# Tokens and the first two weight tiles in quarters, worked off together, with products of ones ahead and squares last

## What is computed

```python
h = rms_norm(x, norm1)                       # over the 2048 columns
z = h @ w_in                                 # 2048 x 5120
u, q, f, i, g = split(z, 1024 columns each)
pool_out = pool_mix(u, ...)                  # windows 2/4/8/16, per-group map, scale
o = hgrn2_recurrence(silu(q), 1 - forget(f), i, log forget(f), state)
x = x + concat(pool_out, norm(o) * silu(g)) @ w_o
h2 = rms_norm(x, norm2)
x = x + (silu(h2 @ w_gate) * (h2 @ w_up)) @ w_down
y = rms_norm(x, norm_f)                      # and the new pooling rows and states
```

## Time and profile before

| | before |
|---|---|
| median of 3 runs | 1475.65 us (1475.46 to 1478.24) |
| profiled execution, its time | 1473.87 us |
| its span, first to last instruction | 1472.1 us |
| PE busy | 1430.2 us, 97% |
| DVE, ACT, POOL busy | 764.2, 575.0, 221.2 us |
| moved by DMA | 214.60 MB, mean 146 GB/s |
| mean granted TensorE clock | 0.988 of full |

### The profile page before, as it was taken

How to read it: one execution, slowest core, us unless ns; L and a number is a source line. 1 busy time by engine, 2 the same in 40 slices (tenths; PEclk the granted TensorE clock), 3 DMA queues, 4 the chain that set the end, 5 groups by cost and what they waited for, 6 DMA issues and landing times.

```text
span 1472.1 us, 26682 instructions
## 1 busy us (share of the span) xinstructions
PE 1430.2 (97%) x9744; PEld 1409.3 (96%) x9744; DVE 764.2 (52%) x1188; ACT 575.0 (39%) x928; POOL 221.2 (15%) x387
## 2 busy tenths in 40 slices
PE   7998999999999999999999999999999999999996
PEld 5998888889999999999999999999999999999996
DVE  5565666667755554444445444444444444444443
ACT  6344445445633343333333333333333333333443
POOL 0263444456312200000000000000000000000131
PEclk9999999999999999999999999999999999999998
DMA  9544445554555555555565554565554556555453
GB/s 247 144 130 132 114 116 144 144 142 121 161 144 142 148 148 151 152 142 134 142 181 142 142 156 124 155 168 146 151 155 125 144 159 171 143 142 149 122 145 111
DMA packets 409521, 214.60 MB, mean 146 GB/s; under 512 B 4093, under 2 KB 407757, under 8 KB 409420
## 3 DMA queue, kind: packets, MB, share of 16 engines
q1 hardware_dynamic: 391207, 203.59, 50.7%
q10 hardware_dynamic: 18277, 10.52, 2.6%
HBM read 206.20 MB, written 7.89 MB: 145 GB/s over the span
## 4 chain that ended last, share of the span: by engine, by line
PE 92%; DVE 3%; POOL 2%; ACT 1%; issue 1%; DMA 1%; DVEq 0%; ACTq 0%; SPq 0%; POOLq 0%
PE bank L382 29%; PE bank L384 29%; PE bank L383 29%; PE bank L522 1%; DVE w_lo L1084 1%; DVE t L1258 1%; DMA xt<-in_x_sample 1%; PE bank L552 1%; PE bank L478 0%; ACT w_hi L711 0%; POOL kp L1606 0%; PE bank L578 0%; ACT tm L849 0%; PE bank L426 0%; POOL km L1597 0%
## 5 line engine op out<-in xcount | busy, mean ns | idle before, releaser
L382 PE MATMUL bank<-a_hi,w_hi 128*128 128x320 f32 x2048 | 641.1, 313 | 0.0
L383 PE MATMUL bank<-a_lo,w_hi 128*128 128x320 f32 x2048 | 636.0, 311 | 0.0
L384 PE MATMUL bank<-a_hi,w_lo 128*128 128x320 f32 x2048 | 635.8, 310 | 0.0
L1084 DVE TENSOR_TENSOR w_lo<-w_raw,w_hi 128x1024 fp32r<-128x1024 f32 (+1 forms) x416 | 459.2, 1144 | 150.8 <-ACT w_hi L711 149.8
L711 ACT ACTIVATE w_hi<-w_raw 128x1024 fp32r<-128x1024 f32 (+1 forms) x416 | 387.9, 968 | 183.2 <-PE bank L384 163.2
L382 PEld LDWEIGHTS bank<-a_hi,w_hi 128*128 128x128 f32 x2048 | 387.4, 189 | 2.1
L383 PEld LDWEIGHTS bank<-a_lo,w_hi 128*128 128x128 f32 x2048 | 387.5, 189 | 0.7
L384 PEld LDWEIGHTS bank<-a_hi,w_lo 128*128 128x128 f32 x2048 | 387.3, 189 | 0.0
L382 PE MATMUL bank<-h_hi,w_hi 128*128 128x320 f32 x704 | 218.5, 310 | 0.0
L384 PE MATMUL bank<-h_hi,w_lo 128*128 128x320 f32 x704 | 217.4, 309 | 0.0
L383 PE MATMUL bank<-h_lo,w_hi 128*128 128x320 f32 x704 | 217.3, 309 | 0.0
(11 more groups left out here) (232 smaller groups left out, 1160.2 us busy)
## 6 DMA issues: line engine op xcount, KB each, us to landing
w_raw<-in_w_gate SPq DMA_DIRECT2D x44, 1024.0 KB, 5.6
w_raw<-in_w_up SPq DMA_DIRECT2D x44, 1024.0 KB, 5.6
w_raw<-in_w_down SPq DMA_DIRECT2D x64, 704.0 KB, 4.8
w_raw<-in_w_in SPq DMA_DIRECT2D x39, 1024.0 KB, 5.8
w_raw<-in_w_o SPq DMA_DIRECT2D x16, 1024.0 KB, 6.1
s<-in_state_hgrn ACTq DMA_DIRECT2D x8, 512.0 KB, 4.8
out<-sn ACTq DMA_DIRECT2D x8, 512.0 KB, 5.2
xt<-in_x_prompt SPq DMA_DIRECT2D x3, 512.0 KB, 9.6
```

The costliest lines, as they stand in the source:

```text
L382: pe.matmul(out, whi[:, par_, cols], r_hi, start=(k == 0), stop=False)
L383: pe.matmul(out, whi[:, par_, cols], r_lo, start=False, stop=False)
L384: last = pe.matmul(out, wlo[:, par_, cols], r_hi, start=False, stop=(k == last_k))
L1084: dve.tensor_tensor(wlo[:, par_, cols], raw[:, par_, cols], whi[:, par_, cols].bitcast(F32), SUB)\
```

## The change

Tokens come in quarters of 512 columns, on twelve semaphores, and the first two weight tiles in quarters of four feature tiles, alternating. PE first multiplies ones by ones (2 products of 512 columns, then, behind the transpose of norm1, 3 more) into a bank nobody reads. Then it turns 3 feature tiles, and works k = 0 to 15 off for units 0 and 1 together, six products for each k. The third token block is padded with zeros (by POOL) to 128 rows, so all three transposes have 128 rows. Units 2 and 3 go to banks of their own (SC, TV), so they need not wait until units 0 and 1 are read; `rms_first` moves to k = 7 of unit 3. The two first squares of ACT move into the k loop (k = 8 and 11), the other four behind it, between the weight halves of units 2 and 3. Weight tile 2 comes in halves, and the cache between them. In the diff, PE waits at k = 0, 4, 8 and 12 for the hi and lo pieces of the quarter; `first_piece` is the piece of 512 columns, on ACT for hi and on DVE in the same place for lo; and the last line is POOL's first. The pooling work from unit 2 on is put in a new written-out order, with the same instructions.

```diff
+            for quarter in range(4):
+                load_x(sp, quarter, 0)
+                if quarter >= 2:
+                    load_x(sp, quarter, 1)
+                for u in range(2):
+                    first_weights(u, quarter)
+            load_params(sp, PARAMS[1:], par_loaded)
+            sp.wait_ge(first_lo, 3)
+            sp.dma_start(w2[:, 0:k_mid, :], win_v[:, 0:k_mid, 2 * P:3 * P]).then_inc(w2_loaded, 16)
             sp.dma_start(cache_t[:, :], cache_pool[0].rearrange("b t c -> (b t) c")).then_inc(cache_loaded, 16)
+            sp.wait_ge(lo_ready, 2)
+            sp.dma_start(w2[:, k_mid:KD, :], win_v[:, k_mid:KD, 2 * P:3 * P]).then_inc(raw_loaded[0], 16)
+            load(3, 1, win_v, (0, KD), 3 * P)
...
-        AHEAD = 8
+        AHEAD = 3
...
-                pe.transpose(b4[:, TP:N], xt[0:NS, 2, k * P:(k + 1) * P], ident[0:NS, 0:NS]).then_inc(xt_t, 1)
+                pe.transpose(b4[:, TP:TP + P], xt[:, 2, k * P:(k + 1) * P], ident).then_inc(xt_t, 1)
+            def keep_busy(count):
+                for _ in range(count):
+                    pe.matmul(OT[:, :].rearrange("p (a b) -> p a b", b=P), ones[:, :],
+                              ones[:, :].unsqueeze(1).to_broadcast([P, 4, P]), start=True, stop=True)
+            pe.wait_ge(fill_done, 1)
+            keep_busy(2)
             pe.wait_ge(ident_loaded, 16)
             pe.wait_ge(norm1_loaded, 16)
             pe.transpose(TK[:, 0:KD], prow[0:KD, :], ident[0:KD, 0:KD]).then_inc(par_t, 1)
+            keep_busy(3)
+            pe.wait_ge(x_pad, 1)
             for k in range(AHEAD):
                 x_transposes(k)
+            for k in range(KD):
                 if k + AHEAD < KD:
                     x_transposes(k + AHEAD)
                 pe.wait_ge(ahi_ready, k + 1)
                 pe.wait_ge(alo_ready, k + 1)
+                for u in range(2):
+                    if k % 4 == 0:
...
+                    out = zb[u][:, 0:N]
+                    pe.matmul(out, whi[:, u, cols], a_hi[:, k, :], start=(k == 0), stop=False)
+                    pe.matmul(out, whi[:, u, cols], a_lo[:, k, :], start=False, stop=False)
+                    last = pe.matmul(out, wlo[:, u, cols], a_hi[:, k, :], start=False, stop=(k == KD - 1))
...
+            unit(U0 + 2, 0, a_rhs, between=(lambda: cache_tiles(0), None), own_bank=SC, read=0)
+            unit(U0 + 3, 1, a_rhs, between=(None, lambda: cache_tiles(1)), after_tile=spread_rms, own_bank=TV, read=0)
+            unit(U0 + 4, 0, a_rhs, between=(fourth_mid, fourth_end), read=1)
...
-            for i in range(2):
-                square(0, i)
+            for u in range(2):
+                first_piece(u, 0)
             act.wait_ge(par_ready, 1)
             for k in range(KD):
...
+                if k % 4 in (1, 2) and k < 12:
+                    first_piece(k % 4 - 1, k // 4 + 1)
                 if k == 8:
+                    square(0, 0)
+                if k == 11:
+                    square(0, 1)
+                if k == 13:
+                    act.wait_ge(w2_loaded, 16)
+                    hi_piece(2, 0, 0, HALF[0])
+            square(0, 2)
+            square(1, 0)
+            act.wait_ge(raw_loaded[0], 32)
+            hi_piece(2, 0, 1, HALF[1])
+            act.wait_ge(raw_loaded[1], 32)
+            hi_piece(3, 1, 0, HALF[0])
+            square(1, 1)
+            square(1, 2)
...
+            pool.memset(xt[NS:P, 2, :], 0.0).then_inc(x_pad, 1)
```

More of the change, by code:

```diff
@@ L30 @@
 HD = D // 2
+QD = D // 4
 TP, NB, TS = 256, 8, 8
@@ L256, in hybrid_kernel @@
         HALF = ((0, 8), (8, 16))
+        QUARTERS = ((0, 4), (4, 8), (8, 12), (12, 16))
         HALF_D = ((0, 8), (8, KB))
@@ L367, in unit @@
             def unit(n, par_, rhs, halves=HALF, between=(None, None), tile_wait=None,
-                     after_tile=None):
-                after(pe, unit_read, n - 1)
+                     after_tile=None, own_bank=None, read=None):
+                after(pe, unit_read, n - 1 if read is None else read)
                 last_k = halves[1][1] - 1
@@ L480, in pool_product, with spread_rms, fourth_mid, fourth_end @@
                     last.then_inc(pool_mm, 1)
[L482 to L498, removed]
+            def spread_rms(k):
+                if k == 7:
+                    rms_first()
+            def fourth_mid():
+                cache_tiles(2)
+                pool_states(0)
+            def fourth_end():
+                pool_states(1)
+                pool_product(0)
+            def sixth_mid():
+                cache_tiles(3)
+                pool_states(2)
+            unit(U0 + 2, 0, a_rhs, between=(lambda: cache_tiles(0), None), own_bank=SC, read=0)
+            unit(U0 + 3, 1, a_rhs, between=(None, lambda: cache_tiles(1)), after_tile=spread_rms, own_bank=TV, read=0)
+            unit(U0 + 4, 0, a_rhs, between=(fourth_mid, fourth_end), read=1)
+            unit(U0 + 5, 1, a_rhs, between=(None, lambda: pool_product(1)), read=2)
+            unit(U0 + 6, 0, a_rhs, between=(sixth_mid, None))
+            unit(U0 + 7, 1, a_rhs, between=(None, lambda: pool_product(2)))
             def sample_thrice(bk, rep):
@@ L714, in _, with first_piece @@
             load_params(act, PARAMS[:1], norm1_loaded)
-            load_x(act, 0, 1)
+            for quarter in range(4):
+                if quarter < 2:
+                    load_x(act, quarter, 1)
+                load_x(act, quarter, 2)
             act.wait_ge(fill_done, 3)
             act.activation(warm[:, 0:1], epst[:, 0:1], ACT.Sqrt)
+            squares = [0]
             def square(half, i):
                 rows, at = (P if i < 2 else NS), 2 * i + half
-                act.wait_ge(x_loaded[half][i], 16)
-                after(act, ss_ready, 3 * half + i)
+                for quarter in range(2 * half, 2 * half + 2):
+                    act.wait_ge(x_loaded[quarter][i], 16)
+                after(act, ss_ready, squares[0])
+                squares[0] += 1
                 act.activation(junk[0:rows, :], xt[0:rows, i, half * HD:(half + 1) * HD], ACT.Square,
                                accum_out=stat[0:rows, at:at + 1]).then_inc(ss_ready, 1)
-            for i in range(2):
-                square(0, i)
+            def first_piece(u, quarter):
+                cols = slice(quarter * QD, (quarter + 1) * QD)
+                act.wait_ge(w_first[u][quarter] if quarter < 3 else raw_loaded[u], 16)
+                ins = act.activation(whi[:, u, cols], raw[:, u, cols], ACT.Copy)
+                if quarter < 3:
+                    ins.then_inc(first_hi, 1)
+                else:
+                    ins.then_inc(hi_ready, 2)
+            for u in range(2):
+                first_piece(u, 0)
             act.wait_ge(par_ready, 1)
@@ L785, in pool_hi @@
                     act.activation(bp_hi[:, j, :], bk[:, 0:N], ACT.Copy, scale=pcol("pool_scale", j)).then_inc(mp_hi_s, 1)
[L787 to L796, removed]
+            cache_copy(0)
+            split_hi(U0 + 4, 0)
+            tail_copy(0)
+            cache_copy(1)
+            split_hi(U0 + 5, 1)
+            cache_copy(2)
+            state_copy(0)
+            tail_copy(1)
+            split_hi(U0 + 6, 0)
+            state_copy(1)
+            pool_hi(0)
+            pool_hi(1)
+            split_hi(U0 + 7, 1)
+            tail_copy(2)
+            cache_copy(3)
+            state_copy(2)
+            split_hi(U0 + 8, 0)
+            pool_hi(2)
             def forget(h, n):
@@ L1134, in lower_bound, with first_piece @@
                 dve.tensor_scalar(lbt[:, 3, :], lbt[:, 4, :], 0.5, 0.5, MUL, ADD).then_inc(lb_ready, 1)
+            def first_piece(u, quarter):
+                cols = slice(quarter * QD, (quarter + 1) * QD)
+                if quarter < 3:
+                    dve.wait_ge(first_hi, 2 * quarter + u + 1)
+                else:
+                    dve.wait_ge(hi_ready, 2 * u + 2)
+                ins = dve.tensor_tensor(wlo[:, u, cols], raw[:, u, cols], whi[:, u, cols].bitcast(F32), SUB)
+                if quarter < 3:
+                    ins.then_inc(first_lo, 1)
+                else:
+                    ins.then_inc(lo_ready, 2)
+            for u in range(2):
+                first_piece(u, 0)
             for k in range(KD):
@@ L1230, in pool_lo @@
                                              in1=bp_hi[:, j, :].bitcast(F32), op0=MUL, op1=SUB).then_inc(mp_lo_s, 1)
[L1232 to L1246, removed]
+            rms_row(1)
+            u_part(0)
+            u_part(1)
+            lo_piece(U0 + 4, 0, 0, HALF[0])
+            u_part(2)
+            lo_piece(U0 + 4, 0, 1, HALF[1])
+            u_part(3)
+            dve.wait_ge(masks_loaded, 16)
+            pool_means(0)
+            lower_bound()
+            split_lo(U0 + 5, 1)
+            pool_means(1)
+            u_part(4)
+            split_lo(U0 + 6, 0)
+            pool_lo(0)
+            u_part(5)
+            pool_lo(1)
+            split_lo(U0 + 7, 1)
+            pool_means(2)
```

(4 more changed lines are left out.)

91 lines of the change are left out of this document (43 added, 48 removed).

## The result

Eight executions of the changed kernel, 1464.65 to 1467.87 us, have a median of **1466.26 us**, against 1475.81 us for eight of before (1471.27 to 1479.33). The ratio is 0.9935, 95% interval 0.9922 to 0.9947: 9.5 us won. The forecast was 1471.4 us and 4.2 us won, in a range from 1466.3.

What follows compares the result with a forecast made beforehand. PE, busy 97% of the span, bounds the kernel. Start 12.7 + loop 19.7 + low clock 2.2 + parameter transpose 0.3 = 34.9 us against 39.05, 4.2 won; on the median of 1475.65 this gave 1471.4 us, range 1466.3 to 1475.0.

Steps and rivals of the forecast that it cites:

- the stalls of the relay: PE waits from a POOL, DVE and ACT relay after a unit is read: six, 15.0 us, and one 4.0; unchanged.
- The mark is 39.05 us: Start of unit 2 in the kernel before, 40.45 us less 1.4 us of PE work that the change moves later.
- its time is 0.12% under the median, and on the median I forecast: Whole kernel: profiled execution 1473.87 us becomes 1469.7; carried to the median of 1475.65, this gives 1471.4 us.
- For as long as in before behind the first product, 4.9 us: Start of the joint loop: low clock level from 12.7 us for 4.9 us, losing 2.2 us.
- the gap before the first product: PE between the ones (over near 9 us) and 12.7 us: only 1.3 to 2.5 us of transposes, so level low.
- Six products are 0.88 + 0.10: Joint k loop: product time per k at full level, 0.10 for the change of kind; a k costs 1.31 us.
- In 8.2 us of transposes alone the level did not rise: Start of the kernel before: 27 transposes ran at the low level, so the low level was assumed at 12.7 us.
- the trace agrees as far as it goes: Start: 27 transposes at the low pace were taken to support the rule that transposes do not count toward full clock.
- the margins at k = 7 of unit 3 and before unit 4: Later units: 3 us spare for 1/rms in unit 3, 0.6 us before unit 4; cost 0, at most 1.
- A: Start: weights land by 9.5 us or the clock carries over; 5.5 to 8 us won, near 1469; chance 0.32.
- B: Start: small transfers run at 190 GB/s, products start at 16.1 us; 0.75 won, 1474.9; chance 0.20 (won under 3).
- C: Later stalls meet other clock moments; three more hit cost 8.7 us against 4.2 won, 1480.1; chance 0.05.

Runs made afterwards that it cites:

- b_same: The kernel before, unchanged, run once more; ratio to before 0.9997.
- a_bridge: The changed kernel with three more products of ones between the transposes of k = 0 and the first joint product; ratio to before 0.9919.
- b_pad: The kernel before with only the third token block padded to 128 rows and its transposes on 128 rows; 1468.58 us, ratio 0.9943.
- a_halves: The changed kernel with tokens and the first two weight tiles in halves, transfers twice as large; ratio to before 0.9957.
- b_ones: The kernel before with only the five products of ones added ahead of the transposes; ratio to before 0.9991.
- b_pad_small: The kernel before with padded transposes and one small 64-row product of ones behind each group of three; 1484.04 us, ratio 1.0047.
- a_rows64: The changed kernel with the third transpose on 64 rows again; ratio to before 0.9953.

## Why the prediction was wrong

Sign and place were right: all that is won is won before unit 2, PE waits nowhere from unit 2 to 7, and the stalls of the relay are the same. The size was not, and four steps have a part in it.

*"The mark is 39.05 us", and "its time is 0.12% under the median, and on the median I forecast".* This step failed most, by 3.5 us. The mark was read from one execution, and I carried its difference to the median, although the start of that kernel depends on when the clock rises. Its start was short because of the very term that the change removes. In b_same the mark is 42.6, and by span and clock 42 of 57 executions go with that trace. Nothing in the one trace said so but a hint that I used the other way round: 27 transposes, and then nine products among further transposes, had passed before the level rose.

*"For as long as in before behind the first product, 4.9 us."* The low level set in at 14 us, not before the first product, and lasted 3.3 us: 1.6 us lost where I had 2.2. That the gap before the first product would cost the level was right (a_bridge fills the gap and keeps it).

*"Six products are 0.88 + 0.10."* The 0.10 for the change of kind was read behind a 64-row transpose. It belongs to the row count: behind padded transposes the first product takes 0.15 us. A k takes 1.21 us instead of 1.31, 1.3 us in thirteen. The padded transposes were right at 0.33.

*"In 8.2 us of transposes alone the level did not rise", and "the trace agrees as far as it goes".* The rule of the Trainium skill ("TensorE: Matmul & The Clock Gate", Part 4), that transposes do not count toward the full clock, does not hold for the float32 transposes of 128 rows here: in b_pad the level rose during transposes alone. The row was read as a statement on all transposes; it was one on groups with a 64-row transpose. So I priced the padding at 0.19 us a group and missed that it gives back a level held low for 15 us or more. It was the part of the change that I gave one sentence.

Right were the first product (12.7 forecast, 13.01 measured), with the slow second weight piece as its cause, that PE sets the pace of the loop, that the margins at k = 7 of unit 3 and before unit 4 hold, and that ones bring nothing over the gap. With pace and level as measured the sum from that trace would have been 5.9 us, inside the range on its own; with the mark of b_same it is 9.5. Of the rivals A came nearest, by neither of its reasons. B was wrong: a_halves shows that smaller transfers win. C did not occur. That the time, 1466.26 us, lies at the very edge of the range is luck: the range was stretched for rival A, not for a baseline that varies.

Not tried: whether 64-row transposes all in a row, with no change of row count, would let the level rise, and whether a small product of 128 rows would hold it down. So why the groups with a 64-row transpose keep it low stays open.

## What to carry to other kernels

Where a profiled stretch runs at TensorE's low level, take a second execution before its length is used in a sum: it may be the part that varies, and a change that ends it wins more than one trace shows. Try equal row counts in a stream of transposes and products; padding 64 rows to 128 took one memset on an idle engine and won 8.4 us here. And an early product is worth more than a warm engine: order the first pieces by when their transfers land.

## What the runs showed that was not expected

- Transposes of 128 rows, nearly back to back, brought TensorE from the low level to the high one: between 9.62 and 15.3 us in b_pad, with no product in between.
- Groups of three with one 64-row transpose went with the low level for 20 us, with PE nearly always busy (b_ones, granted clock 0.50). One added 64-row product for each group of 128-row transposes kept the level low until near 27.6 us (b_pad_small), where b_pad had the high one at 15.3; it cost 15 us, of which 9 or more are the added products.
- A change of row count goes with 0.1 us more in the 64-row transpose and 0.2 us more in the product behind it, at the high level (a_rows64).
- The granted-clock column prints 1.00 until the level first falls from high to low, even while the level is low at the start (b_pad, 10 to 12 us: 1.00, with transposes 0.21 us apart). The pace shows it.
